# Differential scores from stacked high and low parts, and the query and key units put ahead of the second value unit

## The reference

```python
def second_block(...):                     # DEPTH = 2
    for l in range(DEPTH):
        proj = h @ w_in[l]                 # q 512, k 512, v 512, u 512 columns
        q = proj[..., :512].reshape(B, S, 8, 2, 32)
        k = proj[..., 512:1024].reshape(B, S, 8, 2, 32)
        a = diff_attention(q, k, v, lam, lam_init, subln_g[l])
        f = fourier_mix(u, w_f[l], b_f[l])
        h = layer_norm(ALPHA * h + concat(a, f) @ w_o[l], ...)
        h = layer_norm(ALPHA * h + swiglu(h, w_gu[l], w_down[l]), ...)

def diff_attention(q, k, v, ...):
        s = einsum('bqhcd,bkhcd->bhcqk', q, k) * 32 ** -0.5
        s = s - slopes[h] * abs(qpos - kpos)
        p = softmax(s)
        a = p[:, :, 0] - lam * p[:, :, 1]
        o = einsum('bhqk,bkhd->bqhd', a, v)    # then an RMS norm per head
```

## Time and profile before

| | before |
|---|---|
| median of 3 runs, us | 930.98 (930.82 to 931.33) |
| profiled execution, us | 930.78 |
| its span, us | 929.0 |
| TensorE busy, us | 908.2 (98%) |
| VectorE, ScalarE, GpSimd busy, us | 606.7, 474.3, 122.3 |
| loads and stores | 151.6 MB, mean 163 GB/s |
| granted TensorE clock | 0.997 |

### The profile page before, as it was taken

The page is one execution under the profiler, slowest core; times in us unless marked ns, Lnnn a source line. Parts: engine busy times, 40 slices in busy tenths (PEclk is TensorE's granted clock), DMA queues, the critical chain, the costliest instruction groups (busy, mean ns, idle before and its releaser), DMA issues.

```text
span 929.0 us, 13460 instructions
## 1 busy us (share of the span) xinstructions
PE 908.2 (98%) x4958; PEld 765.1 (82%) x4958; DVE 606.7 (65%) x1079; ACT 474.3 (51%) x771; POOL 122.3 (13%) x99
## 2 busy tenths in 40 slices
PE   9999999999999999999999999999999999999996
PEld 6999878889888869887888888877978788888885
DVE  4898677687668585867664545557485965545445
ACT  5855757466785353762543434325574354334430
POOL 5643863102000010002000000000001100000001
PEclk9999999999999999999999999999999999999998
DMA  9654232663533128232465555534332265455521
GB/s 351 229 184 171 92 127 87 217 236 137 210 108 137 58 84 324 94 132 93 176 243 189 179 213 190 177 140 173 146 137 91 100 230 213 176 187 181 188 85 46
DMA packets 22235, 151.59 MB, mean 163 GB/s; under 512 B 2592, under 2 KB 3104, under 8 KB 4256
## 3 DMA queue, kind: packets, MB, share of 16 engines
q1 hardware_dynamic: 20160, 142.62, 42.5%
q10 hardware_dynamic: 2016, 8.16, 2.4%
HBM read 149.72 MB, written 1.05 MB: 162 GB/s over the span
## 4 chain that ended last, share of the span: by engine, by line
PE 86%; DVE 7%; issue 2%; ACT 2%; POOL 1%; DMA 1%; POOLq 0%; DVEq 0%; ACTq 0%; SPq 0%
PE ps L500 15%; PE ps L506 15%; PE ps L502 15%; PE ps L1095 5%; PE ps L531 3%; PE ps L535 3%; PE ps L533 3%; PE ps L775 2%; PE ps L777 2%; PE ps L776 2%; PE ps L551 2%; PE ps L671 2%; PE ps L1113 2%; PE ps L674 1%; PE ps L673 1%
## 5 line engine op out<-in xcount | busy, mean ns | idle before, releaser
L1278 ACT CAST whi<-raw 128x2048 fp32r<-128x2048 f32 (+1 forms) x127 | 241.1, 1905 | 145.5 <-PE ps L506 112.4
L1740 DVE TENSOR_TENSOR wlo<-raw,whi 128x1024 fp32r<-128x1024 f32 x127 | 165.7, 1305 | 141.6 <-ACT whi L1278 141.0
L500 PE MATMUL ps<-whi,ahi 128*128 128x512 f32 (+2 forms) x448 | 173.7, 388 | 0.8 <-issue 0.6
L502 PE MATMUL ps<-wlo,ahi 128*128 128x512 f32 (+2 forms) x448 | 172.0, 384 | 0.0
L506 PE MATMUL ps<-whi,alo 128*128 128x512 f32 (+2 forms) x448 | 171.0, 385 | 0.0
L1746 DVE TENSOR_TENSOR wlo<-raw,whi 128x1024 fp32r<-128x1024 f32 x106 | 129.2, 1218 | 0.0
L500 PEld LDWEIGHTS ps<-whi,ahi 128*128 128x128 f32 x448 | 84.2, 188 | 18.4 <-issue 2.5
L502 PEld LDWEIGHTS ps<-wlo,ahi 128*128 128x128 f32 x448 | 84.2, 188 | 16.5 <-issue 0.5
L506 PEld LDWEIGHTS ps<-whi,alo 128*128 128x128 f32 x448 | 84.1, 188 | 16.3
L531 PE MATMUL ps<-ahi,whi 128*128 128x256 f32 x256 | 73.3, 286 | 0.0
L533 PE MATMUL ps<-alo,whi 128*128 128x256 f32 x256 | 72.4, 283 | 0.0
(11 more groups left out here) (280 smaller groups left out, 1703.6 us busy)
## 6 DMA issues: line engine op xcount, KB each, us to landing
raw<-in_wstream SPq DMA_DIRECT2D x134, 1024.0 KB, 4.8
par<-in_params ACTq DMA_DIRECT2D x5, 1024.0 KB, 4.7
tab<-in_tables ACTq DMA_DIRECT2D x1, 1370.0 KB, 9.5
res<-in_x SPq DMA_DIRECT2D x2, 512.0 KB, 4.4
out<-res SPq DMA_DIRECT2D x4, 256.0 KB, 2.0
par<-in_params ACTq DMA_DIRECT2D x1, 512.0 KB, 3.7
arena<-in_wf ACTq DMA_DIRECT2D x2, 256.0 KB, 4.9
row<-in_rows ACTq DMA_DIRECT2D x1, 176.0 KB, 8.5
```

Source lines behind the costliest of these rows:

```text
L500: pe.matmul(banks[b][:, 0:cw], h_, wh[:, i, c], start=st, stop=False, skip_group_check=True)
L502: pe.matmul(banks[b][:, 0:cw], h_, wl[:, i, c], start=False, stop=False, skip_group_check=True)
L1278: act.copy(whi[:, u % SPL, c], raw[:, u % RAW, c]).then_inc(w_hi, 1)
L1740: dve.tensor_tensor(wlo[:, u % SPL, c], raw[:, u % RAW, c], whi[:, u % SPL, c].bitcast(F32), ALU.subtract).then_inc(w_lo_v, 1)
```

## The change

Queries and keys are now split like the other operands. ScalarE's `qk_out` writes the high part, the new `qk_lo` on VectorE the low part, and `qk_done` (on which side pieces wait for their bank) is counted by `qk_lo`; the columns of the units are reordered, so that a unit's 128 rows are four heads and its two column halves the two components. GpSimd then copies, for every head, three blocks of 32 rows on top of each other into a ring of three stacks (`stack_head`, three transfers of 128 KB a head, 24 a layer): queries high, low, high, and keys high, high, low (`STACKED`). The stacks lie in halves of `bhi` and `blo`, free at that time, and in a widened `wst`. `diff_scores` contracts over the 96 rows, in fp32r, still four matmuls a head, component by component; it waits for `stacked`.

In the stream the second value unit moves behind the four q and k units. Its 8 pieces become side pieces 32 to 39 (56 in all). All 16 pieces of q1 come ahead of the first scores. The copies of v to v2 move into round 1 of VectorE, and `diff_pv(0)` waits for them.

```diff
-        plan += [("vu", l, 0), ("vu", l, 1)] + [("qk", l, i) for i in QK_ORDER]
-        plan += [("vu", l, 2), ("vu", l, 3)]
+        plan += [("vu", l, 0)] + [("qk", l, i) for i in QK_ORDER]
+        plan += [("vu", l, i) for i in range(1, 4)]
...
-D_SPLITS = {0: ("qk", 1), 1: ("qk", 3), 2: ("vu", 2), 4: ("vu", 3), 6: ("w_o", 2)}
+D_SPLITS = {0: ("qk", 3), 1: ("vu", 1), 2: ("vu", 2), 4: ("vu", 3), 6: ("w_o", 2)}
...
-    return (0, 12, 22, 32, 36, 40, 44)[h + 2] if h < 5 else 48
+    return (0, 24, 34, 40, 44, 48, 52)[h + 2] if h < 5 else 56
+FIRST_SCORES = 16
+STACKED = ((0, 0), (1, 0), (0, 1))
+RING = 3
...
+        stack = [s_.rearrange("p k c -> p (k c)").rearrange("p (s c t) -> p s c t", s=2, c=2)
+                 for s_ in (bhi[:, 0:4, :], blo[:, 0:4, :], wst[:, :, :])]
...
+        def stack_uses(l, h):
+            return 16 * len(STACKED) * (l * len(range(h % RING, NH, RING)) + h // RING + 1)
...
                 v_products(0)
                 keep_busy(X[0], 2)
...
-                v_products(1, 0).then_inc(lead_t0, 1)
-                v_products(1, 1).then_inc(w_used, 1)
+                v_products(1).then_inc(w_used, 1)
+                for t in range(T):
+                    wait_emptied(pe, FILL["h", l, t, 1])
                 turned(("qk", l, 0), ahi, alo, G[0])
                 turned(("qk", l, 2), ahi, alo, G[1])
...
                 def diff_scores(h):
                     if h == 0:
-                        pe.wait_ge(qk_done, 4 * l + 2)
                         pe.wait_ge(cw_done, 3 * l + 3)
-                    if h == NH // 2:
-                        pe.wait_ge(qk_done, 4 * l + 4)
-                    if h >= 1:
-                        pe.wait_ge(ds_max, 2 * NH * l + 2 * h)
-                    for t in range(T):
-                        for c in range(2):
-                            n = 2 * h + c
-                            rr = slice(n % 4 * HD, (n % 4 + 1) * HD)
-                            mm = pe.matmul(X[c][:, t * S:(t + 1) * S],
-                                           qkt[rr, n // 4, t * P:(t + 1) * P], qkt[rr, 4 + n // 4, :],
+                    pe.wait_ge(stacked[h % RING], stack_uses(l, h))
+                    rows_ = slice(0, HD * len(STACKED))
+                    q_, k_ = (stack[h % RING][rows_, s, :, :] for s in range(2))
+                    for c in range(2):
+                        if h >= 1:
+                            pe.wait_ge(ds_max, 2 * NH * l + 2 * h - 1 + c)
+                        for t in range(T):
+                            mm = pe.matmul(X[c][:, t * S:(t + 1) * S], q_[:, c, t * P:(t + 1) * P], k_[:, c, :],
                                            start=True, stop=True, skip_group_check=True)
...
                 def diff_pv(h):
                     wait_emptied(pe, FILL["dpt", l, h])
+                    if h == 0:
+                        pe.wait_ge(v_done, T * (l + 1))
...
-                for n in range(3):
+                for n in range(FIRST_SCORES):
                     side_piece(n)
                 diff_scores(0)
-                for n in range(3, side_pieces(-1)):
+                for n in range(FIRST_SCORES, side_pieces(-1)):
                     side_piece(n)
-                pe.wait_ge(v_done, T * (l + 1))
...
                 def qk_out(i):
                     made(act, ("qk", l, i))
                     bank = G[QK_ORDER.index(i) % 2]
+                    dst = qk_part(i, 0).bitcast(F32R)
                     if i < 2:
-                        for j in range(2):
-                            ins = act.activation(qkt[:, 2 * i + j, :], bank[:, j * S:(j + 1) * S], ACT.Identity,
-                                                 scale=const("q_scale")[:, 2 * i + j:2 * i + j + 1])
+                        ins = act.activation(dst, bank, ACT.Identity, scale=const("q_scale")[:, i:i + 1])
                     else:
-                        ins = act.copy(qkt[:, 2 * i:2 * i + 2, :], bank.rearrange("p (k c) -> p k c", k=2))
-                    ins.then_inc(qk_done, 1)
+                        ins = act.copy(dst, bank)
+                    ins.then_inc(qk_hi, 1)
-                split.until(("qk", l, 0))
+                split.until(("qk", l, 3), 0)
                 qk_out(0)
-                split.until(("qk", l, 2))
+                split.until(("vu", l, 1), 0)
                 qk_out(2)
+                split.until(("vu", l, 2), 0)
+                qk_out(1)
...
+                def qk_lo(i):
+                    j = QK_ORDER.index(i)
+                    dve.wait_ge(qk_hi, 4 * l + j + 1)
+                    bank, hi, lo = G[j % 2], qk_part(i, 0), qk_part(i, 1).bitcast(F32R)
+                    if i < 2:
+                        ins = dve.scalar_tensor_tensor(lo, bank, const("q_scale")[:, i:i + 1], hi, ALU.mult,
+                                                       ALU.subtract)
+                    else:
+                        ins = dve.tensor_tensor(lo, bank, hi, ALU.subtract)
+                    ins.then_inc(qk_done, 1)
+                split.until(("qk", l, 3), 0)
+                qk_lo(0)
+                split.until(("vu", l, 1), 0)
+                qk_lo(2)
+                split.until(("vu", l, 2), 0)
+                qk_lo(1)
...
                     if h < NH:
                         combine(h)
+                    if h == 0:
+                        qk_lo(3)
+                    if h == 1:
+                        dve.wait_ge(lead_t0, l + 1)
+                        dve.tensor_copy(v2[:, 0, :], G[2]).then_inc(v_done, 1)
+                        made(dve, ("vu", l, 1))
+                        dve.tensor_copy(v2[:, 1, :], G[3]).then_inc(v_done, 1)
                     if h - 1 in D_SPLITS:
                         split.until((D_SPLITS[h - 1][0], l, D_SPLITS[h - 1][1]))
...
+            def stack_head(l, h):
+                if h == 0:
+                    pool.wait_ge(qk_done, 4 * l + 2)
+                if h == NH // 2:
+                    pool.wait_ge(qk_done, 4 * l + 4)
+                if h >= RING:
+                    pool.wait_ge(ds_psum, 2 * NH * l + 2 * (h - RING) + 2)
+                m, at_ = h % 4, qks_at[h // 4]
+                for b, (fq, fk) in enumerate(STACKED):
+                    first, step_ = 512 * fq, 1024 + 512 * (fk - fq)
+                    src = arena[m * HD:(m + 1) * HD, at_ + first:at_ + first + 2 * step_]
+                    pool.dma_start(stack[h % RING][b * HD:(b + 1) * HD, :, :, :].rearrange("p s c t -> p s (c t)"),
+                                   src.rearrange("p (s x) -> p s x", s=2)[:, :, 0:512]
+                                   ).then_inc(stacked[h % RING], 16)
             for l in range(DEPTH):
+                for h in range(NH):
+                    stack_head(l, h)
```

More of the change, by code:

```diff
@@ L396, in build @@
         r_final = sem("r_final")
-        qk_done, v_done, u_done = (sem("qk_done"), sem("v_done"), sem("u_done"))
+        qk_hi, qk_done, v_done, u_done = sem("qk_hi"), sem("qk_done"), sem("v_done"), sem("u_done")
+        stacked = [sem(f"stacked{r}") for r in range(RING)]
         ds_psum, ds_max, dp_done, da_done = sem("ds_psum"), sem("ds_max"), sem("dp_done"), sem("da_done")
@@ L557, in narrow @@
                 for k in range(KT):
-                    pe.matmul(out, wst[:, k, :], ah[:, k, :], start=(k == 0), stop=False,
+                    pe.matmul(out, wst[:, k, 0:64], ah[:, k, :], start=(k == 0), stop=False,
                               skip_group_check=True)
@@ L1051, in _, with v_products @@
             for l in range(DEPTH):
[L1052 to L1055, removed]
+                def v_products(t):
+                    wait_emptied(pe, FILL["h", l, t, 0])
+                    return tile_products(("vu", l, 0), t, ahi, alo, range(4), 4, 512, [G[2 + t]], True, False)
                 pe.wait_ge(acc_read, 4 * (1 + 2 * l) + 2)
-                v_products(0, 0)
+                v_products(0)
                 keep_busy(X[0], 2)
@@ L1083, in side_piece @@
                     else:
-                        i, t, k = n // 8 % 2, n // 4 % 2, n % 4
-                        name, o = ("vu", l, 2 + i), G[t]
-                        if i == 0 and k == 0:
+                        i, t, k = (n - 32) // 8 + 1, n // 4 % 2, n % 4
+                        name, o = ("vu", l, i), (G[2 + t] if i == 1 else G[t])
+                        if i == 2 and k == 0:
                             pe.wait_ge(qk_done, 4 * l + 3 + t)
@@ L1089, in side_piece @@
                         cc, tt = slice(k * 512, (k + 1) * 512), slice(t * P, (t + 1) * P)
-                        first, last, done = (i, k) == (0, 0), (i, k) == (1, 3), n % 8 == 7
+                        first, last, done = (i, k) == (2, 0), i % 2 == 1 and k == 3, n % 8 == 7
+                        i = i % 2
                         steps = ((ahi[:, 4 * i + k, tt], whi[:, s, cc]),
@@ L1590, in first_hi @@
             def first_hi():
-                split.until(("vu", 0, 1), 0)
+                split.until(("qk", 0, 0), 0)
```

(20 more changed lines are left out.)

20 lines of the change are left out of this document (11 added, 9 removed).

## The result

| | before | after |
|---|---|---|
| median of the runs, us | 930.98 (930.82 to 931.33) | 940.39 (938.5 to 942.5, 4 runs) |
| span of the profiled execution, us | 929.0 | 936.7 |
| TensorE busy, us | 908.2 | 901.3 |
| granted TensorE clock | 0.997 | 0.991 |

The ratio is 1.0101, with a 95% interval of 1.009 to 1.0113. The forecast was 928.1, and 925.0 to 935.5 as the range: the change makes the kernel 1% slower, and the forecast said 0.3% faster.

A forecast was written before the change was run, and what follows sets the result against it. TensorE, on 86% of the chain, was taken as the bound. A gain of 4.1 us a layer less new waits gave +0.15 in layer 0 and -3.0 in layer 1, -2.85 together: 928.1 us, range 925.0 to 935.5.

The forecast's parts named there:

- the landing: Head 0's stack, from the last GpSimd issue to the transfer's arrival: 2.3 us, bounds 2.0 and 6.7.
- the hand-over: Head 0's stack, three issues plus arrival: 5.3 us, bounds 3.0 and 11.7; TensorE waits 2.45 us in layer 0, 1.1 in layer 1.
- rival 5: TensorE's clock falls to half rate in a wait, costing some 4 us: 932 to 933; chance 0.05.
- The wait for q0's bank: Before side piece 0, TensorE waits for VectorE's `qk_lo(0)`: 1.8 us in layer 0, none in layer 1.
- The price of a head's matmuls: Score matmuls in fp32r from 96 rows save 0.74 us a head, bounds 0.58 and 0.78; 5.2 us a layer.
- First Fourier products behind scores 6: After head 6's scores, the first Fourier products come some 1 us later than the 5.05 us of before.
- VectorE's arrears: In the heads, rounds with a split and added copies put VectorE behind: 1.1 us a layer, bounds 0 and 2.9.
- the moved unit: Second value unit, 5.5 us of TensorE work, done between the heads instead of ahead of them: cost nothing.
- Rival 4: GpSimd's issues become the bound, at 1.65 us each in the heads of both layers: 935.2; chance 0.20.
- Rival 3: VectorE's split of unit 6 holds up GpSimd's first issue, hand-over 7.6 us: 932.7; chance 0.10, half of it slower.
- The rule of the Trainium skill: GpSimd cannot write DMA descriptors while VectorE holds the shared port; nothing changes if fp32 subtractions are not in that mode.
- Rival 2: The gain is eaten by a hand-over of 5.8 to 7.6 us, or VectorE's arrears at their bound: 930.9; chance 0.13.

The follow-up runs named there:

- Experiment 3: Changed kernel with SyncE holding the load of the fourth value unit, and all behind it, until head 0's stack has landed; 932.38 us, ratio 1.0012.
- experiment 4: Changed kernel with the stacks' destination declared fp32, so that the transfers copy and do not convert; 941.53 us, ratio 1.0109.
- experiment 5: Kernel before with only the score matmuls changed to fp32r over 96 rows, without stacks, transfers or low parts; 923.46 us, ratio 0.9912.
- experiment 9: Changed kernel with ScalarE's two u2 copies moved ahead of the four exponentials of head 6 in round 5; 935.62 us, ratio 1.0052.
- experiment 8: Changed kernel with all 32 pieces of the second q and k units ahead of scores 0, 11.5 us of cover instead of 5.8; 937.91 us, ratio 1.0062.
- experiment 7: Changed kernel with bit-copy transfers, head 0's three issued from ScalarE's queue instead of GpSimd's; 945.63 us, ratio 1.0169.
- experiment 2: Changed kernel with the loads of the norm parameters issued in round 3 of the heads, not ahead of q0; 934.75 us, ratio 1.0041.
- experiment 6: Changed kernel without GpSimd's transfers: ScalarE writes high parts into the stacks, scores 0 wait only for k0's low part; 927.45 us, ratio 0.9954.
- experiment 10: Changed kernel with three weight loads a layer each held until a stack has landed, and 6 more pieces ahead of scores 0; 931.38 us, ratio 1.0003.
- experiment 1: Changed kernel with four dummy fp32 matmuls ahead of TensorE's wait for head 0's stack in each layer; 939.79 us, ratio 1.0079.

## Why the prediction was wrong

**The step that failed is a term, the landing in "the hand-over is 3 x 1.0 + 2.3 = 5.3 us".** The two numbers in it were wrong in opposite directions. An issue of GpSimd took 0.50 to 0.77 us, not 1.0. The last landing took 6.22 and 5.85 us, not 2.3. The whole hand-over came to 7.9 and 7.4 us, not 5.3. I had both bounds, 2.0 and 6.7, and chose "with 128 KB the row for 256 KB is nearest", that is by size. But the row for 256 KB is the store of the output at the end, where nothing else is in flight; the 6.7 is of this very stretch. The nearest row was the one with the same company, though that it fits so well is partly chance: the last transfers of head 1 took 10.25 and 9.45 us beside the same loads. With 6.7 my own sum would have been 3.0 + 6.7 = 9.7, twice 3.0 over the point at which the change is even: slower. Experiment 3 shows the cause (2.77 us with a weight load held) and refutes a fixed cost of the software queue; experiment 4 excludes conversion. The waits were 4.73 and 4.04 us instead of 2.45 and 1.1, 5.2 us more. Some 0.8 of that is not the hand-over's: in layer 1 TensorE was there 3.4 us behind `qk_lo(2)`, where the sum had 4.15.

**The second step is rival 5, the clock, at 0.05.** I looked at the waits that I expected, 1.8 and 2.45 us, and not at those within my bounds. At 4.73 and 4.04 us the clock fell in both, and also behind the 2.5 us in front of layer 1's Fourier products, but not behind the equal wait in layer 0. That is 2.45 + 1.6 + 1.7 = 5.8 us. With the 5.2 above it is 11.0; the spans were off by 7.7 + 2.85 = 10.6. The two don't add up exactly, and as the clock was not tried apart, its share is read from the trace and not shown by a run. The remaining 1.7 us between the profiled execution and the median of after is in runs that were not profiled: the changed kernel spreads over 4.0 us, the one before over 0.5. A fall that comes in one execution and not in the next would do that. The clocks of the runs agree with it: 938.5, 939.27, 941.52 and 942.5 us came with a mean granted clock of 0.991, 0.988, 0.987 and 0.986. Where the further falls were is not known, as those runs have no trace.

**What was right.** The wait for q0's bank: 1.83 us, in layer 0 only (1.8 forecast), put down to VectorE. Scores as four records, 0.48 us; rounds of 4.59 (402.63 - 398.04) against 4.63. The price of a head's matmuls (0.74 us) fits these rounds and experiment 5. That experiment 5 as a whole gave 7.6 us against my 8.2 is in part luck, as it has other losses in it than I had summed. First Fourier products behind scores 6: 6.2 us against 5.05 before, about 1 later as said, but the size came right for a reason that I did not have: ScalarE's order sets most of it (experiment 9 takes 2 us of the wait away). VectorE's arrears are there too: in layer 1 the chain runs over VectorE from 679.3 to 696.0 before it reaches ScalarE. Their share was not measured. No later head waited for its stack, but nearly: experiment 8. Whether the moved unit cost anything beyond the wait for q0's bank was not tried apart.

**The other rivals.** Rival 4 (GpSimd's issues as the bound) is refuted, at 0.5 us an issue. Rival 3 too: VectorE made its split of unit 6 from 363.90 to 366.26 while GpSimd issued from 364.30 on, and the issues beside it (0.77, 0.50, 0.54 us) were hardly longer than those behind it (0.51 to 0.54), without a gap. The rule of the Trainium skill, "SBUF — State Buffer", in the box on how the vector engine can hold up a DMA, does no harm here: these fp32 subtractions are not seen to hold up anything. Its advice, another queue, made this kernel slower (experiment 7, 945.63 against 941.53 for the same copies in experiment 4), with the transfers of heads 1 and 2 issued beside it. Rival 2 was the right mechanism, up to 7.6 us of hand-over, and too cheap, as it had no clock in it.

Of the transfer time the Trainium skill, "DMA: Bandwidth & Descriptors", in the section on the anatomy of one DMA on the software path, gives a fixed 2.0 us and the bytes at 436 GB/s: 2.3 us for 128 KB, called an estimate. The trace agrees with it where the queues are quiet (2.3 to 3.2 us for heads 4 and 5 of the changed kernel), and not where weights are in flight (4.8 to 10.2 us for heads 0 to 3, up to 15.46 in experiment 3).

## What to carry to other kernels

Price a new transfer by the landings of the stretch in which it will run, not by those of its size, and look up what was issued just before it: here weight units of 1 MB, and parameters that could be moved out of the way at no cost (experiment 2, faster than the changed kernel). Test a new wait of TensorE at its bound for what the half rate behind it would cost, not only at the value taken: in this kernel that was as much as the waits' own excess. When a wait is covered by moved work, look at the next consumer of the same queue: covering head 0 uncovered head 1, and delaying the weights starved round 3.

## What the runs showed of the hardware

- A 128 KB copy between buffers of SBUF beside 1 MB loads and other such copies took 4.8 to 10.2 us from its issue to its landing (heads 0 to 3 of the changed kernel), where it took 2.3 to 3.2 with no load in flight (heads 4 and 5), and up to 15.46 in a burst of three loads (experiment 3). The last ones on ScalarE's queue took 9.2 and 8.5.
- GpSimd issued such a transfer in 0.50 to 0.55 us (0.77 and 0.62 for the first of a layer), also while VectorE subtracted fp32 operands in SBUF.
- The clock did not fall in step with the longest wait. It fell in waits of 4 us, but also near waits of 1.8 to 2 us in experiments 5 and 6 and at one of 0.82 (with one of 0.75 shortly before it) in experiment 10, and not behind a wait of 1.83 followed by full work, nor behind 2.55 us in layer 0 of the changed kernel, nor behind 3.0 in layer 0 of experiment 8. Dummy matmuls in the wait did not prevent it in layer 0; in layer 1 no fall came there (experiment 1). Why one fell and the other not is open.
